# Blocked triangular inverse: the transposed copy made by transposing the corrected one, in place of a product for its own correction

## The reference, cut to what matters

```python
    a_mat = jnp.where(strict, jnp.einsum("bhncd,bhnsd->bhncs", k_beta, k) * decay, 0.0)
    eye = jnp.eye(CHUNK, dtype=q.dtype)
    t_mat = lax.linalg.triangular_solve(eye + a_mat, jnp.broadcast_to(eye, a_mat.shape),
                                        left_side=True, lower=True)
    u = jnp.einsum("bhncs,bhnse->bhnce", t_mat, v * beta[..., None])
    w = jnp.einsum("bhncs,bhnsd->bhncd", t_mat, k_beta * jnp.exp(g)[..., None])
```

## Time and profile before

| | before |
|---|---|
| median of three runs | 1717.1 us |
| profiled execution | 1709.29 us |
| its span | 1707.4 us |
| PE busy | 1502.6 us (88%) |
| DVE busy | 1093.1 us (64%) |
| POOL busy | 797.2 us (47%) |
| ACT busy | 554.4 us (32%) |
| mean granted PE clock | 0.935 |

### The profile page before, as it was taken

One profiled execution on the slowest core, in us unless ns is written; L12 is line 12 of the kernel. 1 busy time (PEld: TensorE's weight loads), 2 busy tenths in 40 slices (PEclk: granted clock), 3 DMA queues, 4 the chain that ended last, 5 costly groups with the idle time before them and its releaser, 6 DMA issues.

```text
span 1707.4 us, 23446 instructions
## 1 busy us (share of the span) xinstructions
PE 1502.6 (88%) x9034; PEld 1113.6 (65%) x9034; DVE 1093.1 (64%) x2121; ACT 554.4 (32%) x782; POOL 797.2 (47%) x746
## 2 busy tenths in 40 slices
PE   7999999775665699999878967989999999999999
PEld 6997676663211266666333432449999985699999
DVE  4855654689488877876856665237775436567753
ACT  6652111211221222232000011236654524466542
POOL 0024230276778766656677777624552101125630
PEclk9999999997877799999999997998999999989999
DMA  7437780498999999999999999985554525735550
GB/s 274 149 130 296 275 300 25 145 401 309 386 407 368 409 390 401 402 403 403 407 404 402 403 386 408 408 301 187 198 177 152 191 100 197 278 120 196 195 176 26
DMA packets 154255, 477.23 MB, mean 280 GB/s; under 512 B 10016, under 2 KB 12320, under 8 KB 150944
## 3 DMA queue, kind: packets, MB, share of 16 engines
q0 software_dynamic: 73728, 268.47, 40.2%
q1 hardware_dynamic: 80416, 207.27, 33.3%
HBM read 474.65 MB, written 1.05 MB: 279 GB/s over the span
## 4 chain that ended last, share of the span: by engine, by line
PE 59%; DMA 12%; DVE 9%; POOL 9%; issue 4%; ACT 1%; DVEq 0%; ACTq 0%; POOLq 0%
PE ps L666 59%; DMA arena<-in_peer_v,cl 9%; POOL arena L2723 7%; DVE arena L1802 2%; DMA wring<-in_peer_v,cl 2%; POOL wring L2723 1%; DVE arena L1419 1%; DVE arena L1425 1%; PE ps L670 1%; DMA wring<-in_peer_u,arena 1%; DMA wring<-in_ada 1%; DVE wring L1802 0%; DVE arena L1732 0%; DVE pr L1422 0%; DVE arena L1422 0%
## 5 line engine op out<-in xcount | busy, mean ns | idle before, releaser
L666 PE MATMUL ps<-arena,wring 128*128 128x256 f32 (+2 forms) x2360 | 600.1, 491 | 103.2 <-DMA arena<-in_peer_v,cl 97.7
L666 PEld LDWEIGHTS ps<-arena,wring 128*128 128x128 f32 (+1 forms) x2360 | 332.0, 167 | 352.6 <-DMA arena<-in_peer_v,cl 175.5
L1802 DVE CUSTOM_DVE_ANT_0 arena<-arena 128x1024 f32<-128x1024 f32 x214 | 257.5, 1226 | 136.0 <-DMA arena<-in_peer_u,arena 132.7
L2723 POOL DMA_INDIRECT arena<-in_peer_u,arena x214 | 240.8, 1125 | 190.9 <-DVE arena L1760 79.3
L2723 POOL DMA_INDIRECT arena<-in_peer_v,cl x214 | 226.7, 1059 | 78.9 <-issue 58.2
L2130 ACT ACT_TABLE_LOAD x64 | 82.1, 1283 | 395.2 <-DVE arena L1802 265.5
L1419 DVE TENSOR_TENSOR wl<-wring,wh 128x2048 fp32r<-128x2048 f32 (+1 forms) x76 | 167.8, 2208 | 60.7 <-ACT wh L2133 58.6
L666 PE MATMUL ps<-hh,wh 128*128 128x256 f32 x704 | 202.1, 287 | 3.9 <-DVE hl L1425 3.9
L666 PE MATMUL ps<-hl,wh 128*128 128x256 f32 x704 | 201.6, 286 | 0.0
L666 PE MATMUL ps<-hh,wl 128*128 128x256 f32 x704 | 201.6, 286 | 0.0
L1425 DVE SCALAR_TENSOR_TENSOR cvb<-ps,vec,cvb 128x255 f32<-128x255 f32 x264 | 127.5, 483 | 92.5 <-ACT cvb L2130 85.2
(11 more groups left out here) (261 smaller groups left out, 2327.1 us busy)
## 6 DMA issues: line engine op xcount, KB each, us to landing
wring<-in_ups SPq DMA_DIRECT2D x33, 2048.0 KB, 10.7
wring<-in_ada SPq DMA_DIRECT2D x24, 2048.0 KB, 8.5
wring<-in_ffn_w_down SPq DMA_DIRECT2D x12, 2048.0 KB, 8.3
wring<-in_w_in SPq DMA_DIRECT2D x8, 2048.0 KB, 8.2
wring<-in_ffn_w_down SPq DMA_DIRECT2D x6, 1536.0 KB, 8.3
wring<-in_peer_wq SPq DMA_DIRECT2D x4, 2048.0 KB, 14.6
wring<-in_attn_w_qkv SPq DMA_DIRECT2D x4, 2048.0 KB, 8.4
wring<-in_w_out SPq DMA_DIRECT2D x2, 2048.0 KB, 8.4
```

The lines of the kernel that those rows point to most:

```text
L666: return pe.matmul(o, l, r, start=start, stop=stop)
L1802: ve.tensor_tensor_reduce(out=o, in0=o, in1=h2[:, t, :], scale=1.0, scalar=0.0, op0=MUL, op1=ADD, accum_out=dots[j % 2][:, k:k + 1]).then_ ...
L2723: po.indirect_dma_start(out=ring[n % NR], out_offset=None, in_=table, in_offset=bass.IndirectOffsetOnAxis(ap=which, axis=0)).then_inc(S[f" ...
```

## The change

Part 1 of levels 1 to 5 has only `lc`. In part 0 of levels 2 to 6, before `la`, PE transposes the four corrected matrices of the head into a PSUM bank (`lt`), after a wait for `v_dd` of the level before, and ACT copies them into `DT` (signal `a_lt`), before its copy of `la`. Part 1 waits for `a_lt` also. Level 6 keeps `lb` and its subtraction. Signals are renumbered to fit.

```diff
@@ PE
                 else:
-                    pe.wait_ge(*at("v_dt", n - 4))
+                    pe.wait_ge(*at("v_dd", n - 4))
+                    b = take(("lt", n - 4), "a_lt", n - 4)
+                    for i in range(4):
+                        k = tr(b[:, c128(i)], DD[:, 4 * h + i, :])
+                    k.then_inc(S["p_lt"], 1)
                 b = take(("la", n), "a_lx", n)
...
             pe.wait_ge(*at("a_lx", n))
+            if l > 1:
+                pe.wait_ge(*at("a_lt", n - 4))
             if l < 6:
                 b = take(("lc", n), "v_dd", n)
...
-            b = take(("lb", n), "v_dt", n)
-            for i in range(4):
-                k = mm(b[:, c128(i)], X[:, 4 * h + i, :], DT[:, 4 * h + i, :], True, True)
-            k.then_inc(S["p_lb"], 1)
+            else:
+                b = take(("lb", h), "v_dt", h + 1)
+                for i in range(4):
+                    k = mm(b[:, c128(i)], X[:, 4 * h + i, :], DT[:, 4 * h + i, :], True, True)
+                k.then_inc(S["p_lb"], 1)
@@ DVE
-            ve.wait_ge(*at("p_lb", n))
-            told(tt(flat(heads4(DT, h)), flat(heads4(DT, h)), where["lb", n], SUB), "v_dt", n)
+            else:
+                ve.wait_ge(*at("p_lb", h + 1))
+                told(tt(flat(heads4(DT, h)), flat(heads4(DT, h)), where["lb", h], SUB), "v_dt", h + 1)
@@ ACT
+                else:
+                    ac.wait_ge(*at("p_lt", n - 4))
+                    told(copy(flat(heads4(DT, h)), where["lt", n - 4]), "a_lt", n - 4)
                 ac.wait_ge(*at("p_la", n))
                 told(copy(flat(heads4(X, h)), where["la", n]), "a_lx", n)
```

More of the change, by code:

```diff
@@ L109, in program @@
         "p_cu": ("p_mb", 8), "p_cd": ("p_dec", 8), "p_dn": ("p_cd", 24), "p_ckv": ("p_ms", 4), "p_hs": ("p_ckv", 3),
-        "p_vt": ("p_lb", 24), "p_s": ("p_cu", 22), "p_pt": ("p_q", 10), "p_o": ("p_sc", 10), "p_y": ("p_o", 8),
+        "p_lb": ("p_lt", 20), "p_vt": ("p_lb", 4), "p_s": ("p_cu", 22), "p_pt": ("p_q", 10), "p_o": ("p_sc", 10), "p_y": ("p_o", 8),
         "p_hb": ("p_wo", 4), "p_hr": ("p_pl", 4), "p_wd": ("p_crs", 3), "p_mrs": ("p_wd", 4),
@@ L115, in program @@
         "a_gp": ("a_c16", 1), "a_gl": ("a_gp", 1), "a_eg": ("a_gl", 1), "a_em": ("a_eg", 1), "a_h2T": ("a_em", 1), "a_xc": ("a_h2T", 4),
-        "a_sz": ("a_crs", 3), "a_mrs": ("a_sz", 1), "v_mrc": ("v_rq", 2), "p_mrb": ("p_l2b", 4), "a_go": ("a_vn", 4)}
+        "a_lt": ("a_dd", 4), "a_sz": ("a_crs", 3), "a_mrs": ("a_sz", 1), "v_mrc": ("v_rq", 2), "p_mrb": ("p_l2b", 4), "a_go": ("a_vn", 4)}
     class Signals(dict):
@@ L938, in _ @@
             pass
-        pe.wait_ge(*at("v_dt", 24))
+        pe.wait_ge(*at("v_dt", 4))
         pe.wait_ge(*at("g_bv", 4))
```

## The result

| | before | changed |
|---|---|---|
| median of six runs | 1714.59 us (1707.73 to 1718.49) | 1700.04 us (1697.85 to 1702.67) |
| profiled execution, its span | 1709.29 us, 1707.4 us | 1700.78 us, 1699.0 us |

The ratio is 0.9924, with a 95% interval of 0.9906 to 0.9942. Of 1714.59 us that is 13.0 us less, 10 to 16; the two medians as they stand differ by 14.6 us. The direction was right, but 1700.04 us lies under the range of 1703 to 1716. The median of before has moved too: three further runs brought it from 1717.1 to 1714.59 us.

The account below looks back on a forecast made before the run. PE's own work was taken to bound the loop; 1.8 us (eight mLSTM steps) + 6.5 (other steps) + 0.3 (conditioning wait) = 8.6 us, passed on in full from the 1717.1 us median to 1708.5 us, range 1703 to 1716.

Parts of the forecast that it names:

- the cold stretch: Lower PE clock (0.79) at 292 to 300 us, behind the loop; may fall otherwise when shifted, 1 us either side.
- What bounds the kernel: In the loop of 48 steps PE's own work is the bound, plus 3.8 us of waits.
- The cost of a group: On PE in the loop, four products cost 0.89 us, four transposes 0.455 us including 0.02 for switching; 20 groups each.
- the bounds of 4.8 to 9.6: Loop gain: 7.8 to 9.1 us before waits, less at most 3 us for new waits, plus at best 0.5 us.
- The mLSTM chain: Between a head's two `mo`, a 4.75 us chain limits PE's saving; eight steps gain 1.8 us in sum.
- Rival A: The mLSTM chain and ACT's in-order queue eat more, banks may come free late; gain 4.8 us or less, chance 0.14.
- the conditioning wait: PE's 0.48 us wait for the conditioning copy in step 27 shrinks, a gain of 0.3 us.
- ACT's room: ACT has room for 20 more copies, 11.9 us; bare part 0 takes PE 5.4 us and ACT 5.0 us.
- Does it reach the end: Behind the loop, later work and loads shift along, so the 8.6 us pass through in full.
- B: Rival: no gain, 1717 us, because something doesn't move with the loop or transposes cost what products cost; chance 0.07.
- C: Rival: transposes and idle time in the loop drop PE's clock to 1.2 GHz, up to 1740 us; chance 0.04.
- D: Rival: transposes cheaper than the rows show, or luck in the cold stretches' shift; 10 to 13 us gained, chance 0.10.

Follow-up runs that it names:

- The identity products: The changed kernel with each transpose written as a plain fp32 product with the identity: loop 118.40 us, median 1725.4 us, ratio 0.9998 to the kernel before.
- the pads: The changed kernel plus idle products: 40 behind the loop, ratios 0.9997 and 0.998; 160 there, 1.0166; 40 in the second feed-forward layer, 0.9989.
- after_again: The changed kernel repeated without edit, with its own profile: 1712.81 us, ratio 0.9926 to the kernel before on the same chip.
- after_third: The changed kernel repeated without edit on the third chip: 1700.28 us, ratio 0.9939 to the kernel before on that chip.
- all four pairs: The unedited changed kernel against the kernel before, the first measurement and three repeats: ratios 0.9924, 0.9926, 0.9939 and 0.9930.
- the five other kernels of the same loop: The changed kernel with idle products added (four runs) or its copies on DVE; ratios with added length taken off 0.9945, 0.9927, 0.9937, 0.9957, 0.9943.

## Why the prediction was right and wrong

The mechanism was right: PE's own work bounds the loop, transposes are cheaper than products, and the loop's gain reaches the end. The step that failed is the last one, from the loop to the timed median. It subtracted 8.6 us from 1717.1 us, a median of three runs, and let such a median move by "some 2 us" and the cold stretch by 1 us. That median alone moved by 2.5 us, and the medians of six runs differ by 14.6 us where the loop gave 9.4. A smaller error in the same direction is a term of the sum, the 0.455 us for a group of transposes, which measured 0.42.

- *What bounds the kernel.* Right: PE's own work, in a loop that it fills. The identity products take the whole gain back.
- *The cost of a group.* This is the term of the loop's sum that was mis-sized. A removed group is 0.89 us, as said. An added group of transposes was put at 0.455, as if the switch between kinds of work came on top. The rows show 0.44 in the bare steps (243.55 to 243.99), and between two conditionings `lt` and `la` hold PE from 227.75 to 229.23, 1.48 us, where `la` alone took 1.09 (240.07 to 241.16 before): 0.39 us for the group, which fits a switch that was paid ahead of `la` before as well and is now paid once by both. With waits equal, 20 x 0.89 - 9.43 = 8.4 us for 20 groups, 0.42 each. The loop's 9.43 us lie inside the bounds of 4.8 to 9.6, but only by the 0.5 us allowed for shorter waits: the waits did not change, and PE's work alone was to give at most 9.1. The Trainium skill's factor of four for FP32 ("TensorE: Matmul & The Clock Gate", section "Terms") is not what the rows show against a product: 0.435 against 0.89 us a group, a factor of two.
- *The mLSTM chain.* Right in kind: the wait of step 10 went (forecast), 0.54 us came at step 4 (forecast 0.6). At step 16 a wait of about 1.2 was forecast and 1.48 stood there: the chain was taken with a mask of 0.69 us, as at head 3, and at this step DVE's mask took 1.08 us beside POOL's masking (0.87 in the kernel before). At step 22 the forecast 0.6 us ahead of `mo` was taken by 0.48 us for a bank one step earlier, after which `mo` waits for nothing. Rival A named banks, but the sum looked at none there. That the waits still come to 3.85 us, where the forecast ones would make about 3.9, is in part luck: the bank and the longer mask stand in for the 0.6 us at step 22 and for what was to be left of the conditioning wait.
- *ACT's room.* Right: PE waits for no copy of ACT in the loop of the changed kernel, and moving the 20 copies to DVE changes nothing.
- *Does it reach the end.* One to one, as the pads show. But the prediction let the cold stretch behind the loop count 1 us to either side. Its rows cost 1 to 1.7 us, and ten idle products there moved the timed median by 5.5 us (interval 2 to 9), so that the term was too small. From the loop's end to the last instruction the changed kernel took 2.1 us more in the first pair of profiles, and 3.2 and 3.1 us less in the pairs after_again and after_third (1461.9 against 1465.1, 1446.9 against 1450.0).
- *The final number.* It stood on a median of three runs, 1717.1; six gave 1714.59. Of the distance between forecast (1708.5) and result (1700.04), 8.5 us, that is 2.5, the loop's size is 0.8, and 5.1 us are excess and scatter in that comparison. Over all four pairs the ratio has a mean of 0.9930, 12.0 us, so 2.6 us beyond the loop; with the five other kernels of the same loop 1.5 us. What this rest is, is not settled.
- *The range* failed because it was built from the mechanism's bounds and 2 us of scatter. The runs of the kernel before on one chip spread over 11 to 21 us, those of the changed kernel over 5 to 10, and both medians have an error.
- *Rivals.* A (less than 4.8 us) and B (nothing) are out. C is out: the clock is 1.00 at 220 to 230 and at 240 to 252 us with transposes among the products. Its price was also added up wrongly: 40 us on 1708.5 are 1748.5, not 1740. D (10 to 13 us gained) comes nearest: the gain of 13.0 us by the ratio is at its edge, though 1700.04 us lies under its 1704 as well. Its first half is true by 0.7 us (20 x 0.035); of its second, a cold stretch that falls otherwise, the first two profiles show nothing: both have that stretch, with ways of 65.0 and 65.5 us. On rival C the Trainium skill ("TensorE: Matmul & The Clock Gate", "Part 4: PE-mode transpose") has the rule that transpose mode does not count as busy for the clock gate. With products between the transposes it cost nothing here, the clock of 1.00 above; no run has transposes alone for long.

## What to carry to other kernels

When a transposed copy of a matrix is kept by a second product, price a transpose against the product row by row: here one fp32 transpose has one row where a product has two, and one correction with a transpose behind it takes 1.3 us where two corrections take 1.8. Where PE is the bound, the copy out of PSUM may sit on ACT or on DVE, whichever has room at that step; here both gave the same loop. Then read the short waits that are left, name for each whether it is data or a bank, and fill them by moving other work by a step; that brought the first gather another 3.7 us forward. A forecast of 0.5% needs more than a median of three runs to stand on, and a range that holds the error of both medians.

## What the runs showed of the hardware

- An fp32 transpose of 128 x 128 takes PE 0.109 us among its like; as a product with the identity it takes 0.22.
- Transposes alternating with products, one third of the groups of level 6, left the granted clock at 1.00 (240 to 252.1 us).
- PE's wait of 2.46 us was followed by a window of 1.2 GHz in 11 of 15 profiles. With 2.2 us of idle products in it none of the three profiles had one there, and the kernel before got faster by 0.32% (interval 0.12 to 0.51) though its work grew.
- DVE's masking of 128 x 512 took 0.69 us in every step in which POOL did nothing beside it. With POOL's masking beside it it took 0.87 to 1.22 us in three of the five such steps of the kernel before, and 0.69 in the other two; in the changed kernel 1.19, 1.08, 0.80 and 0.69 us.
